# Attention layer of a decoder trunk: value units among the query units, halves swapped by the scalar engine, 16 partitions per sample, and idle matmuls over two waits

## The chip, the cores and the metric

The kernel runs on one core of one Trainium2 chip. A core has TensorE (PE: matmuls and transposes, results in PSUM), VectorE (DVE), ScalarE (ACT), GpSimd (POOL) and SyncE (SP, here only a queue that issues DMAs). Each runs its own instructions in order; they meet at semaphores. The metric is the device time in microseconds (us) of one launch; lower is better.

## The reference

One inference step of a two-layer decoder trunk, for a prompt of 256 tokens and 8 samples with one new token each. The kernel holds both as one set of 264 columns (T = 256 + 8). Layer 0 mixes tokens by sparse attention, layer 1 by a recurrent block; after each comes a gated MLP with a short convolution. Cut to the attention that the change touches:

```python
q, k, v, qi, ki, wi = split(a @ w_in)         # 8 heads of 128; indexer: 4 heads of 64, one key of 64
q, k, qi, ki = rope(q), rope(k), rope(qi), rope(ki)
# rope: x1, x2 = halves of a head; [x1*cos - x2*sin, x2*cos + x1*sin]
score = sum_h relu(qi_h . ki) * wi_h          # causal for the prompt; 257 keys for a sample
idx = top_k(score, 64)
o = softmax(q . k[idx] / sqrt(128)) @ v[idx]  # a sample takes its keys from a paged cache in DRAM
h = h + o @ w_out
```

For the prompt the kernel computes all logits and masks those that are not selected. For a sample it gathers 64 rows of the key cache and 64 of the value cache, and treats the new token's own key apart.

## The kernel before

Weights are float32 in DRAM. A unit is one 1024x128 block of a weight matrix (512 KB): SP loads it into one of four stages, ACT makes its float16 high part (`hi`, w_hi, L498), DVE the rest (`lo`, w_lo, L796), and PE multiplies 8 chunks of 128 rows by the 264 columns, three matmuls a chunk (L1263 to L1265; L1352 to L1354 where two or three units go chunk by chunk together), into PSUM bank u % 4. Stage, parts and bank are freed four units later, so load u waits for w_lo of u - 4, w_hi of u for unit u - 4, and unit u for the reader of bank u - 4.

The attention layer has 27 units in the order of `ORDER`: two of index queries (i0, i1), one of the index key and weights (w0), 8 of queries (q), 8 of keys (k), 8 of values (v). All but the value units are roped. DVE reads the bank three times (L882: times cos into its place; L884 and L886: each half times sin into the other half of `rot`; index units have four such halves), and POOL adds the two (L1658, semaphore roped). A value unit is copied by ACT (L589, L590).

All engines run a loop over u, and the work beside the units is hung into it by hand, by unit number. In this order:

- POOL issues 16 gathers of cached index keys (`kx`, L1593), sets constants, and only then begins the additions. After unit 4 PE waits for three roped units and computes the index scores (L1376 to L1391); after unit 6 it transposes the index keys.
- DVE sums the weighted scores (L1004, L1010) and takes the 64 largest in eight rounds of eight: `take_second` for tokens 128 to 255 (L896, L897), `take_merged` for the others and the samples, with indices (L902 to L904). At u = 12 it turns the samples' indices into cache row numbers (to L1037, semaphore phys_done). PE transposes them (L1425), DVE casts them (gix), and POOL gathers cached keys and values (L1651).
- SP writes the samples' queries to DRAM (L422) and reads them back broadcast over partitions (L380), 64 partitions a sample, two samples in a tile, in a buffer for two tiles; tiles 2 and 3 wait until DVE has read tiles 0 and 1. `sample_dots` (L929, L931, L933) multiplies them by the gathered keys and sums, at u = 16 to 19. PE transposes the dots after unit 19 (L1446).
- The prompt's heads start at LG = 17, one head a unit: logits on PE (L1322, L1323), masked row maximum on DVE (L914), exponentials on ACT (L560), normalising on POOL (L1671), transposes (L1329 to L1331) and output (L1339, L1340) on PE, output split on ACT and DVE (L571, L923). `TURNS` says after which unit a roped key or a value head is transposed for the store (L1313, L1314; kept by ACT, L580).
- The samples' value sums are PE's L1461, 8 matmuls a unit after units 22 to 25, with `pb`, the weights, two columns a tile; L1464 sums the weights. Then come the 8 units of w_out from 193.35 us.

Much later, after the 16 units of w_rec_in, the recurrent block's end makes z in 8 chunks (zH on ACT, zL on DVE, L1193), and the first two w_rec_out units take them chunk by chunk (L1352).

## Time and profile before

| what | value |
|---|---|
| time, median of 3 runs (lowest to highest) | 680.48 us (679.82 to 681.27) |
| the profiled execution: its time, its span | 684.84 us, 683.0 us |
| mean granted clock of TensorE | 0.933 |
| busy: PE, DVE, ACT, POOL | 598.2, 480.5, 350.5, 275.8 us |
| DMA | 115.42 MB, mean 169 GB/s |
| share of the chain that ended last: PE, DVE, issue, POOL, DMA | 56%, 17%, 14%, 5%, 4% |

The span runs from the first to the last instruction of the profiled execution. Busy time of PE is not PE at its peak, since matmuls are pipelined; the time between the starts of two matmuls says more than the length of one. The granted clock is 1.00 at full speed and 0.50 at half.

### The profile page before, as it was taken

The page shows a single profiled execution, that of the slowest core. Times are in us where ns is not written, and L with a number is a line of the kernel's source. Part 1 is how long each engine was busy: PE and PEld are TensorE (multiplying, and loading weights), DVE is VectorE, ACT ScalarE, POOL GpSimd, SP SyncE. Part 2 cuts the span into 40 slices and gives each one's busy share as a digit, 9 for nine tenths or more (in the row PEclk, how much of TensorE's full clock was granted, in tenths as well). Part 3 has the DMA queues.
Part 4 walks back from the last instruction along what each step waited for, and adds up shares of the span by engine and source line. Part 5 has one row for each costly group of instructions (what it writes and reads, how often), then busy time and mean ns, then how long its engine had stood idle before and what let it go on. Part 6 is the DMA issues. An engine that isn't in the chain of part 4 may idle for free.

```text
span 683.0 us, 12723 instructions
## 1 busy us (share of the span) xinstructions
PE 598.2 (88%) x5020; PEld 510.8 (75%) x5020; DVE 480.5 (70%) x876; ACT 350.5 (51%) x568; POOL 275.8 (40%) x275
## 2 busy tenths in 40 slices
PE   6869357369979999999999998948999999999995
PEld 5647246249867888888888887746888888888885
DVE  4569974576439888887865568797988778885442
ACT  6414204136427766665654458954776656663322
POOL 5843316127313354455400139983245545440001
PEclk9869759769999999999999999986999999999999
DMA  8833329913327876666876555542667666679601
GB/s 246 233 94 98 92 63 283 272 31 95 92 67 269 252 208 195 192 200 194 256 213 202 141 154 155 147 131 66 194 202 202 200 191 198 202 225 254 173 10 64
DMA packets 206076, 115.42 MB, mean 169 GB/s; under 512 B 5769, under 2 KB 202489, under 8 KB 205993
## 3 DMA queue, kind: packets, MB, share of 16 engines
q1 hardware_dynamic: 203601, 108.46, 56.1%
q0 software_dynamic: 2048, 5.79, 2.6%
q8 instruction: 40, 0.66, 0.4%
q10 hardware_dynamic: 368, 0.35, 0.2%
q14 instruction: 19, 0.16, 0.1%
HBM read 110.94 MB, written 3.90 MB: 168 GB/s over the span
## 4 chain that ended last, share of the span: by engine, by line
PE 56%; DVE 17%; issue 14%; POOL 5%; DMA 4%; ACT 4%; POOLq 1%; SPq 0%; ACTq 0%; DVEq 0%
PE acc L1263 16%; PE acc L1264 16%; PE acc L1265 16%; DVE w_lo L796 4%; DMA scratch<-q_rows 3%; POOL area L1593 3%; ACT w_hi L498 1%; DVE area L1179 1%; DMA pt<-in_page_table 1%; PE acc L1352 1%; DVE area L929 1%; DVE aL L803 1%; PE acc L1353 1%; PE acc L1354 1%; PE misc L1461 1%
## 5 line engine op out<-in xcount | busy, mean ns | idle before, releaser
L1263 PE MATMUL acc<-aH,w_hi 128*128 128x264 f16 (+1 forms) x1032 | 288.4, 279 | 1.1 <-DVE aL L803 0.8
L1264 PE MATMUL acc<-aL,w_hi 128*128 128x264 f16 (+1 forms) x1032 | 288.4, 279 | 0.0
L1265 PE MATMUL acc<-aH,w_lo 128*128 128x264 f16 (+1 forms) x1032 | 288.2, 279 | 0.0
L796 DVE SCALAR_TENSOR_TENSOR w_lo<-stage,w_hi 128x1024 f16<-128x1024 f32 (+1 forms) x179 | 235.0, 1316 | 52.8 <-ACT w_hi L498 52.2
L498 ACT ACTIVATE w_hi<-stage 128x1024 f16<-128x1024 f32 (+1 forms) x179 | 196.9, 1101 | 85.1 <-PE acc L1265 78.4
L1263 PE MATMUL acc<-zH,w_hi 128*128 128x264 f16 x440 | 121.5, 276 | 0.0
L1264 PE MATMUL acc<-zL,w_hi 128*128 128x264 f16 x440 | 121.4, 276 | 0.0
L1265 PE MATMUL acc<-zH,w_lo 128*128 128x264 f16 x440 | 121.4, 276 | 0.0
L1263 PEld LDWEIGHTS acc<-aH,w_hi 128*128 128x128 f16 (+1 forms) x1032 | 102.7, 99 | 19.2 <-issue 1.6
L1264 PEld LDWEIGHTS acc<-aL,w_hi 128*128 128x128 f16 (+1 forms) x1032 | 102.3, 99 | 17.6 <-issue 0.3
L1265 PEld LDWEIGHTS acc<-aH,w_lo 128*128 128x128 f16 (+1 forms) x1032 | 102.3, 99 | 16.3
L1647 POOL TENSOR_TENSOR scratch<-work,r0z 128x264 f32<-128x264 f32 x44 | 65.5, 1489 | 80.2 <-ACT work L700 80.2
L1645 POOL COPY ftail<-scratch 128x10 f32<-128x10 f32 x44 | 47.0, 1068 | 35.5 <-DVE scratch L1105 35.3
L1658 POOL TENSOR_TENSOR area<-area,scratch 128x264 f32<-128x264 f32 x16 | 26.4, 1649 | 73.2 <-DVE scratch L886 73.2
L695 ACT ACTIVATE work<-scratch,fprm 128x264 f32<-128x264 f32 x44 | 26.7, 607 | 52.0 <-DVE scratch L1105 51.8
L1263 PEld LDWEIGHTS acc<-zH,w_hi 128*128 128x128 f16 x440 | 43.0, 98 | 6.7 <-DVE w_lo L796 0.3
L1265 PEld LDWEIGHTS acc<-zH,w_lo 128*128 128x128 f16 x440 | 43.1, 98 | 6.4
L1264 PEld LDWEIGHTS acc<-zL,w_hi 128*128 128x128 f16 x440 | 43.1, 98 | 6.3
L1105 DVE TENSOR_TENSOR scratch<-acc,rinv 128x264 f32<-128x264 f32 x44 | 19.0, 432 | 39.5 <-PE acc L1265 39.4
L1577 POOL TENSOR_TENSOR sqsum<-sqsum,sq 128x264 f32<-128x264 f32 x21 | 16.8, 800 | 68.0 <-ACT sq L510 68.0
L700 ACT ACTIVATE work<-work 128x264 f32<-128x264 f32 x44 | 18.6, 423 | 34.9 <-DVE work L1116 34.9
L506 ACT ACTIVATE aH<-hT,gcol 128x264 f16<-128x264 f32 x24 | 12.3, 513 | 37.7 <-DVE hT L1135 23.2
(340 smaller groups left out, 742.4 us busy)
## 6 DMA issues: line engine op xcount, KB each, us to landing
stage<-in_w_ffn_up SPq DMA_DIRECT2D x88, 512.0 KB, 4.6
stage<-in_w_ffn_down SPq DMA_DIRECT2D x32, 704.0 KB, 5.0
stage<-in_w_attn_in SPq DMA_DIRECT2D x26, 512.0 KB, 4.3
stage<-in_w_rec_in SPq DMA_DIRECT2D x16, 512.0 KB, 4.0
stage<-in_w_attn_out SPq DMA_DIRECT2D x8, 512.0 KB, 3.7
stage<-in_w_rec_out SPq DMA_DIRECT2D x8, 512.0 KB, 3.7
scratch<-q_rows SPq DMA_DIRECT2D x8, 256.0 KB, 8.1
area<-in_x_prompt SPq DMA_DIRECT2D x2, 512.0 KB, 4.7
```

The costliest lines, as they stand in the source:

```text
L498: nc.scalar.activation(w_hi[:, s, 0:n, 0:cols], stage[:, s, 0:n, 0:cols], ACT.Copy, scale=WSCALE).then_inc(hi_done, 1)
L695: nc.scalar.activation(c32[:, p, :], gs[:, p, :], ACT.Identity, scale=fprm[layer][:, FROW_W + 2, j:j + 1], bias=fprm[layer][:, FROW_B, j:j ...
L700: nc.scalar.activation(c32[:, p, :], c32[:, p, :], ACT.Gelu_apprx_tanh).then_inc(gelu_done, 1)
L796: v.scalar_tensor_tensor(w_lo[:, s, 0:n, 0:cols], stage[:, s, 0:n, 0:cols], WSCALE, w_hi[:, s, 0:n, 0:cols], ALU.mult, ALU.subtract).then_ ...
L1105: v.tensor_tensor(gs[:, p, :], acc[:, u % 4, 0:T], rinv[:], ALU.mult).then_inc(acc_read, 1)
L1263: t_.matmul(out, w_hi[:, s, c, 0:cols], xH[:, x0 + c, :], start=first and c == 0, stop=False)
L1264: t_.matmul(out, w_hi[:, s, c, 0:cols], xL[:, x0 + c, :], start=False, stop=False)
L1265: ins = t_.matmul(out, w_lo[:, s, c, 0:cols], xH[:, x0 + c, :], start=False, stop=last and c == n - 1)
L1593: g.indirect_dma_start(out=kx[:, page, s * ID:(s + 1) * ID], out_offset=None, in_=kidx_rows, in_offset=bass.IndirectOffsetOnAxis(ap=gidx[: ...
L1645: g.tensor_copy(ftail[:, :, j], gs[:, p, TP - 2:T]).then_inc(tail_copied, 1)
L1647: g.tensor_tensor(gr[:, p, :], c32[:, p, :], r0z[:], ALU.mult).then_inc(gr_done, 1)
L1658: g.tensor_tensor(dst, dst, rot[0:part, (before(u) + 1) % 2, :], ALU.add).then_inc(roped, 1)
```

## The change

The core of the diff, by engine; the renumbering of steps that only move with the unit order is left out.

Order and buffers:

```diff
-ORDER = ("i0 i1 w0 q0 q1 q2 q3 q4 q5 q6 q7 "
-         "k0 v0 k1 k2 v1 k3 k4 v2 k5 k6 k7 v3 v4 v5 v6 v7").split()
+ORDER = ("i0 i1 w0 q0 q1 v0 q2 q3 v1 q4 q5 v2 q6 q7 v3 "
+         "k0 k1 k2 k3 k4 k5 k6 k7 v4 v5 v6 v7").split()
-TURN_K = (14, 15, 17, 18, 20, 21, 22, 28)
-TURNS = sorted([(U_V[h] + 1, "v", h) for h in range(H)] + [(TURN_K[h], "k", h) for h in range(H)])
+TURN_K = (17, 18, 19, 20, 21, 22, 23, 28)
+TURN_V = (8, 12, 13, 15, 24, 25, 26, 27)
+TURNS = sorted([(TURN_V[h], "v", h) for h in range(H)] + [(TURN_K[h], "k", h) for h in range(H)])
-        qb = scratch[:, 0:2048].rearrange("p (j d) -> p j d", j=2)
+        qb = scratch[:, 0:1024]
-        pb = sb("pb", [P, 4, H, 2])
+        pb = sb("pb", [P, 4, H, NS])
```

A sample now has 16 partitions, and its 64 keys lie in 4 tiles of 16; so one broadcast of all 8 queries serves all tiles. SP issues weight loads 4 to 6 ahead of the 21 parameter rows:

```diff
+            for u in range(4, 7):
+                load_in(u)
...
-            for u in range(4, U_OUT):
+            for u in range(7, U_OUT):
...
-                if u == 21:
+                if u == 23:
                     sp.wait_ge(smp_kept, 1)
                     sp.dma_start(q_rows, smp[:, 0, :]).then_inc(q_out, 16)
                     sp.wait_ge(q_out, 16)
-                    for j in range(2):
-                        broadcast_q(j)
-                if u in (24, 25):
-                    sp.wait_ge(qb_read, u - 23)
-                    broadcast_q(u - 22)
+                    sp.dma_start(qb, q_rows.rearrange("(s h) d -> s (h d)", h=H).unsqueeze(1).to_broadcast([NS, 16, D])).then_inc(qb_in, 16)
```

ACT swaps the halves, after the head's steps of that u and ahead of `hi(u + 4)`; DVE multiplies in place:

```diff
+            def swap_halves(u):
...
+                act.wait_ge(unit_done, u + 1)
+                if r > 2:
+                    act.wait_ge(roped, r - 2)
+                for b in range(0, rows_n, 2 * half):
+                    nc.scalar.copy(rot[b:b + half, r % 2, :], acc[b + half:b + 2 * half, s, 0:T])
+                    ins = nc.scalar.copy(rot[b + half:b + 2 * half, r % 2, :], acc[b:b + half, s, 0:T])
+                ins.then_inc(swapped, 1)
...
-                v.tensor_tensor(dst, acc[0:rows_n, s, 0:T], cos[0:rows_n, :], ALU.mult)
-                for b in range(0, rows_n, 2 * half):
-                    v.tensor_tensor(rot[b:b + half, r % 2, :], acc[b + half:b + 2 * half, s, 0:T],
-                                    sin[b + half:b + 2 * half, :], ALU.mult)
-                    ins = v.tensor_tensor(rot[b + half:b + 2 * half, r % 2, :], acc[b:b + half, s, 0:T],
-                                          sin[b:b + half, :], ALU.mult)
-                ins.then_inc(acc_read, 1)
+                dve.wait_ge(swapped, r)
+                v.tensor_tensor(rot[0:rows_n, r % 2, :], rot[0:rows_n, r % 2, :], sin[0:rows_n, :], ALU.mult)
+                v.tensor_tensor(dst, acc[0:rows_n, s, 0:T], cos[0:rows_n, :], ALU.mult).then_inc(acc_read, 1)
```

DVE's steps: the wait for three roped units and the placing of the index queries (`qz`, 4 copies instead of 8) come ahead of rope 3 instead of behind w_lo 7. Score sums go to u = 7, `take_second` to u = 8 (3 rounds), 9 and 10 (2 each) and 15 (1), `take_merged` to u = 11 to 14 (2 rounds each), the row numbers to u = 14, `sample_dots` from 16 to 19 to 18 to 21. `lane` and `own` are two new reduces of the identity at u = 5. Addresses and weights:

```diff
+                    small(v.tensor_tensor(picked.rearrange("p (n r) -> p n r", r=16), C[:, 0:P].rearrange("p (n r) -> p n r", r=16),
+                                          lane[:].unsqueeze(1).to_broadcast([P, 8, 16]), ALU.mult))
+                    small(v.tensor_reduce(gbias[:], picked.rearrange("p (n r) -> p n r", r=16), AX.X, ALU.add))
+                    v.tensor_copy(gix[:], gbias[:, 0:4]).then_inc(gix_done, 1)
...
+                    v.tensor_tensor(pb[:].rearrange("p j h s -> p (j h) s"), E[:, 0:32].unsqueeze(2).to_broadcast([P, 32, NS]),
+                                    own[:].unsqueeze(1).to_broadcast([P, 32, NS]), ALU.mult)
```

PE: idle matmuls (`keep_warm`, whose result nobody reads), the first two units staggered, and the value sums:

```diff
+            keep_warm(acc[:, 2, 0:P], 14)
+            for c in range(DC):
+                a_ready(0)(c)
+                chunk(0, c, aH, aL)
+                if c in (0, 1):
+                    keep_warm(acc[:, 2, 0:P], 4)
+                else:
+                    chunk(1, c - 2, aH, aL)
...
-                if u == 12:
+                if u == 15:
...
+                    t_.matmul(C[:, 0:P], of_sample[:], pf, start=True, stop=True).then_inc(phys_turned, 1)
...
-                if 22 <= u < 26:
-                    j = u - 22
+                if u in (24, 25):
                     pe.wait_ge(pb_done, 1)
...
+            pe.wait_ge(gate_tanh, 2 * DC)
+            keep_warm(A[:, 0:P], 80)
             units_together(U_ROUT, 2, zH, zL, lambda c: pe.wait_ge(y_lo, c + 1))
```

The other steps on PE move with them: index scores from after unit 4 to after 5, key transposes from 6 to 7, sample scores from 7 and 8 to 9 and 10, parameter transposes from 9 to 11, the dots' transposes from 19 to 21.

POOL sets its constants first, gathers 8 of the 16 index key pages, and issues the other 8 in pairs after additions 1 to 4; the key and value gathers move from u = 13 to 16 to u = 16 to 19:

```diff
+            gather_index_keys(0, 8)
...
+                if 1 <= u < 5:
+                    gather_index_keys(6 + 2 * u, 2)
-                if 13 <= u < 17:
-                    pool.wait_ge(gix_done, 2)
+                if 16 <= u < 20:
+                    pool.wait_ge(gix_done, 1)
```

## Rows read from the trace of the kernel before

**Rows 1.** Busy time by stretch: PE, PEld, DVE, ACT, POOL; clock, DMA, GB/s.

```profile
0.00:44.50 44.50, 29.36 (x197) 24.41 (x198) 25.80 (x53) 19.96 (x36) 28.21 (x39) 0.81 0.75 208
44.50:93.30 48.80, 29.21 (x227) 22.80 (x226) 42.65 (x112) 13.23 (x21) 14.23 (x8) 0.78 0.36 94
93.30:145.30 52.00, 30.09 (x205) 24.19 (x205) 31.24 (x61) 13.78 (x29) 19.51 (x17) 0.76 0.73 197
145.30:193.35 48.05, 43.29 (x334) 37.76 (x334) 26.59 (x90) 23.10 (x67) 19.14 (x29) 0.93 0.27 79
```

**Rows 2.** Instructions in order of time on PE: start us, length us, line, tiles.

```profile
160.61 0.39 PE L1322 MATMUL misc<-area 128*128 128x128 f32 x2
160.83 0.60 PE L1323 MATMUL misc<-area 128*128 128x256 f32 x2
...
473.27 0.28 PE L1263 MATMUL acc<-zH,w_hi 128*128 128x264 f16 x1
473.38 0.28 PE L1264 MATMUL acc<-zL,w_hi 128*128 128x264 f16 x1
```

**Rows 3.** PE's waits from 0 to 200 us: total us, times, longest.

```profile
PE misc L1322 <- DVE nmx L914: 18.5, 2, 11.1
PE misc L1425 <- DVE zL L1037: 12.8, 1, 12.8
PE misc L1376 <- issue: 7.7, 1, 7.7
```

**Rows 4.** Groups of POOL, 0 to 200 us: busy us, mean ns, idle before.

```profile
L1658 POOL TENSOR_TENSOR area<-area,scratch 128x264 f32<-128x264 f32 x16 | 26.4, 1649 | 73.2 <-DVE scratch L886 73.2
L1593 POOL DMA_INDIRECT area<-in_cache_kidx,gidx x16 | 19.1, 1196 | 4.9 <-issue 4.6 <-POOL gidx L1588 0.3
```

**Rows 5.** Instructions in order of time, all engines, near 35 us.

```profile
34.91 1.44 POOL L1658 TENSOR_TENSOR zH<-zH,scratch 128x264 f32<-128x264 f32 x2
35.76 0.42 DVE L882 TENSOR_TENSOR zH<-acc,ca 64x264 f32<-64x264 f32 x1 [5.81 <-POOL zH L1658]
```

**Rows 6.** Groups of ACT, 0 to 200 us.

```profile
L498 ACT ACTIVATE w_hi<-stage 128x1024 f16<-128x1024 f32 (+1 forms) x31 | 32.4, 1044 | 48.2 <-PE acc L1265 41.5 <-DMA stage<-in_w_attn_in 6.7
L560 ACT ACTIVATE work<-work,nmx 128x128 f32<-128x128 f32 (+1 forms) x16 | 7.1, 449 | 32.5 <-DVE nmx L914 32.5
L590 ACT ACTIVATE scratch<-acc 128x264 f32<-128x264 f32 x8 | 3.1, 382 | 0.0
```

**Rows 7.** The tile q_rows: its DMA issues, and time to landing.

```profile
L380 SPq DMA_DIRECT2D scratch<-q_rows x8: 445/596/3477, 105.7 to 126.7; - x8
...
DMA to landing us min/median/max: 3.6/7.8/10.2
```

**Rows 8.** Groups of DVE from 52.6 to 93.3 us.

```profile
L796 DVE SCALAR_TENSOR_TENSOR w_lo<-stage,w_hi 128x1024 f16<-128x1024 f32 x7 | 8.6, 1226 | 0.2
...
L884 DVE TENSOR_TENSOR scratch<-acc,ca 64x264 f32<-64x264 f32 x6 | 2.6, 434 | 0.1
...
L896 DVE MAX8 top<-zH 128x8 f32<-128x256 f32 x6 | 2.6, 427 | 0.2
```

**Rows 9.** Groups of all engines from 97 to 145 us.

```profile
L929 DVE TENSOR_TENSOR area<-scratch,area 128x1024 f32<-128x1024 f32 x4 | 5.4, 1356 | 12.4 <-DMA scratch<-q_rows 12.4
...
L931 DVE TENSOR_REDUCE qk<-area 128x8 f32<-128x1024 f32 x4 | 4.9, 1220 | 0.1
```

**Rows 10.** Instructions in order of time on PE, value sums and last wait.

```profile
162.25 1.84 PE L1461 MATMUL misc<-pb,area 128*128 128x2 f32 x16
...
191.59 0.48 PE L1313 MATMUL misc<-ca,scratch 128*128 128x128 f32 x1 [4.16 <-DVE zL L923]
```

**Rows 11.** Instructions in order of time on PE, first output unit of the recurrent block.

```profile
463.23 0.40 PE L1352 MATMUL acc<-zH,w_hi 128*128 128x264 f16 x1 [10.83 <-DVE zL L1193]
463.43 0.43 PE L1353 MATMUL acc<-zL,w_hi 128*128 128x264 f16 x1
463.65 0.43 PE L1354 MATMUL acc<-zH,w_lo 128*128 128x264 f16 x1
```

**Rows 12.** Instructions in order of time on DVE, the last two parts zL.

```profile
468.69 1.00 DVE L1193 TENSOR_TENSOR zL<-work,zH 128x264 f16<-128x264 f32 x2
```

More of the change, by code:

```diff
@@ L1276, in _ @@
             pe.wait_ge(ones_set, 1)
-            for _ in range(WARM):
-                t_.matmul(acc[:, 0, 0:P], ones[:], ones[:], start=True, stop=True)
+            keep_warm(acc[:, 0, 0:P], WARM)
             pe.wait_ge(const_in, 16)
```

260 lines of the change are left out of this document (131 added, 129 removed).

## The prediction

> **What bounds the kernel now.** I read the busy time by stage first [rows 1]. From 193 us on (both FFN layers and the recurrent block) TensorE, PE from here, is busy nearly without a break at full clock, but for one hole near 460 us. The attention layer, the first 193.35 us, is different: PE is busy 29 us of each of its first three stretches of 44 to 52 us, and its mean clock there is 0.76 to 0.81. Its 27 projection units need 24 matmuls each at 0.11 us [rows 2], 2.7 us a unit, 73 us in all; the rest of the stage is waiting. PE's waits name what for [rows 3]: 7.7 us before the transposes of L1376 (the third rope), 12.8 us for the gather addresses that VectorE (DVE) works out (L1037), 18.5 us for the row maxima of the logits (L914), which stand behind the query-key products on DVE's queue. So three chains in a row set the stage: GpSimd (POOL) at the start, DVE from 45 to 93 us, then a DMA and DVE up to the transposes of the dots at 145.3 us. The change shortens each; I follow them as clock readings and compare with those of before.
>
> **Start, to the index matmuls.** POOL issues 16 gathers of index keys at 1.2 us, plus 0.3 us between two, before it does anything else [rows 4]; they hold it from 9.6 to 33.3 us, the rope additions queue behind them, and DVE's third rope starts at 35.76 [rows 5]. With 8 gathers it is free near 21.8. The idle matmuls hold PE's first unit to a steady start at full clock, where they now run partly at half clock; a float matmul of 128 columns takes 0.22 us warm (two instructions between 160.61 and 160.83) [rows 2], so 14 of them end at 14.9, 4 and 4 more at 16.1 and 17.3, and the first two units end at 21.0 and 22.0, not 23.1: 1 us earlier.
> A rope before is three DVE instructions of 0.43 us beside one POOL addition; after, ScalarE (ACT) copies the two halves crosswise out of PSUM and DVE does two. The nearest row for a copy is the value units' one of 128x264, 0.38 us, the next instruction following 0.27 us later [rows 6]. I take 0.27 a copy: 0.55 us for a query or key unit, 1.1 us for an index unit, done before the weight split w_hi, 1.04 us in the mean and 0.95 to the next instruction, on the same queue. So unit end to rope end goes from 1.34 to 0.6 + 0.9 = 1.5 us, but DVE's own share falls from 1.34 to 0.89. Bounds for a copy: 0.27 and 0.38 us if each waits for the last; I keep both for the range, plus more in a rival.
> Then: first rope done on DVE 23.7, second 25.8, third 27.9; POOL adds them at 24.4, 27.5 and, after two gathers (2.5 us, the time of two late ones), 30.75. Before, the third was added at 38.9. DVE now waits at this point ahead of rope 3 and its w_lo; they end at 34.7, and unit 7, which needs that w_lo, starts at 37.8, so nothing is late. Index matmuls: from 32.8 (unit 5 is done by then) to 34.9 at full clock, against 44.46 with one unit less done. Parameter rows now go out behind three weight loads: load 7 leaves at 25.3 instead of well before; its w_hi is wanted at 31, and it lands near 30.
> The new wait is for the index keys themselves: the last two gathers go out behind rope additions 3 and 4 and their issue ends at 40.8, landing near 43 (my estimate is 2 us; the nearest row, the query rows' way to DRAM and back, gives 3.6 as the shortest [rows 7], so 44.5 is the upper bound); PE is there at 40.5. So 2.5 us idle; unit 8 ends at 47.2.
>
> **Selection, to the gather addresses.** This is DVE alone: busy 42.65 of 48.8 us before [rows 1]. From its rope at 52.65 to the addresses at 93.0 it works 40.4 us. After: five ropes of 0.89 instead of six of 1.34 (-3.6), one w_lo of 1.15 more, one selection round more (two DVE instructions, 0.99), one flag and one doubled address less (-0.35): 38.6 us [rows 8]. It starts at 41.2 and waits once, 1 us, for unit 8's w_hi; the addresses stand at 81.0, against 93.3. PE idles from 70.8 to 81.0 and restarts at half clock, as it does before in the stretch after 93.3 (mean clock 0.76 [rows 1]); I charge unit 16 with 5.4 us. The two reduces for lane and own fall into a gap of DVE at 38 us; each is under one 256-wide selection instruction (0.43 us), so without that gap they cost 0.3 to 0.9 us.
>
> **Query broadcast and dots.** The new form needs one product, one reduce and one cast of at most 128 columns (0.8 us, between two and three times 0.43) for the addresses and one broadcast for all samples. Load 23 waits for w_lo 19, done 82.4; the query rows leave at 83.0, land 3.6 us later, and the single 512 KB broadcast goes out at 86.8. Before, eight of 256 KB took 7.8 us in the median and up to 10.2 to land [rows 7], and the second half waited for a free buffer. I take 7.8 us, the median: 94.6. Bounds: 5 and 10.2 us; DVE comes to it only at 97.6, after logits 0 and rope 18, so only the upper one can touch it. Key rows are issued at 90.2 and land near 98.5. From there DVE goes round one loop per unit: logits 0.55, ACT's exponentials 0.9 and swap 0.55, rope 0.9, w_lo 1.15 to the next instruction (1.23 by itself), dots 1.23 + 1.22 + 0.2 [rows 6, 8, 9], 6.9 us with gaps. Here the swap is a cost: it stands behind the exponentials on ACT, and DVE's rope behind it. Four rounds: the last dot at 122.0. PE waits 3 to 5 us in each round, hidden behind DVE. So the transposes move from 145.3 to 122.1; this piece is 41.1 us instead of 52.0.
> The Trainium skill speaks against the one broadcast: its page DMA: Bandwidth & Descriptors, section Rules for kernel authors, says that an outermost dimension under 16 confines a DMA to that many engines, and this source has 8 outermost. By it the transfer runs on half the engines; no row of before has such a shape (those broadcasts have 64 outermost), so this is a rival below.
>
> **Tail.** Two units fewer are left (5, not 7): -5.4 us. Unit 22 is now a key unit, so PE waits 2 us at the token-major transpose for the output split behind rope 22. The value sums: 32 matmuls of two instructions over two units instead of four, 64 instructions either way (16 take 1.84 us with the last one's latency [rows 10]), and six more instructions for the weight sum, 0.7 us; the wider N is free. From unit 26 to the last head nothing is touched: the wait of 4.16 us before 191.59 stays [rows 10]. Readings: units 22, 23, 24, 25, 26 end at 128.4, 134.9, 140.2, 148.3, 156.9; output projection at 164.0, not 193.35. That piece is 41.9 instead of 48.05.
>
> **Recurrent output.** PE waits there 10.83 us and resumes at 463.23, at half clock (0.2 us a matmul) [rows 11]. The change puts 80 float matmuls there, 80 x 0.22 = 17.8 us warm, from 452.2 to 470.0. The last zL is done at 469.7 [rows 12], so all eight chunks are then ready: 48 x 0.112 = 5.4 us, the pair ends at 475.4 instead of 473.27. PE has no gap behind it for 200 us, so +2.1 us stay. Bounds: +1.6 if a pass takes 0.107 us, and -2.9 if the idle matmuls ended before the first zL: the chunks would then keep pace with the zL, and the pair end 0.7 us after the last of them, at 470.4.
> The Trainium skill's page TensorE: Matmul & The Clock Gate, section Why this matters for your kernels, says to leave no idle gap between bursts, which taken alone gives a gain here. The row bears out the half clock after the gap, but not that filling it past its end is free: that rule gives -2.9, my sum +2.1.
>
> **Sum.** Addresses -12.3, broadcast and dots -10.9, tail -6.1, idle matmuls +2.1: -27.2 us. The profiled execution spans 683.0 us and took 684.8, 4.4 above the median of 680.5; so the -27.2 us are applied to the median: 653.3 us.
>
> **Rivals.** (1) Less comes through, 662 us: the POOL-DVE pair slows both (a POOL addition takes 1.65 us in the mean and 0.72 alone [rows 4, 5]), rope's first product now has both operands in SBUF, and each of the four rounds and some of the first units lose 1 to 1.5 us, some waits push PE to half clock at unit 8. For: such additions overlap w_lo often. Against: DVE's own rows hardly stretch. (2) The broadcast on half the engines (the first page named above would have it): twice the longest landing, 20.4 us, gives 107 instead of 98.5, 662 us. Against: it goes out while the DMA queues are light, and twice the median is 102, +4. (3) More comes through, 647 us: the idle matmuls pay (-2.9) or the rounds run nearer 6 us since exponentials overlap. (4) Slower than before, 690 us: ACT's queue becomes the ring. A swap waits for the rope two before, and w_hi stands behind it; if copies between partition halves cost over 1.0 us each, then 19 units lose 1.4 us each and the gain is gone. That is the point; at 1.3 us it is 690. Against: 0.38 us in the only such row, though between the same partitions. (5) The edits hide behind each other and nothing moves, 680: would need the selection chain to start no earlier, against the 7.7 us wait.
>
> **How the numbers follow.** Forecast 0.58; (1) 0.13; (2) 0.08; (3) 0.16; (4) 0.04; (5) 0.01. The predicted time is the forecast's, 653.3 us. The range takes in (1), (2) and most of (3) and the bounds of copies and landing: 643 to 665. Faster by over 0.2% (about what a measurement of this kernel can tell from no change) 0.95, same 0.01, slower 0.04.
>
> **What would show it.** In the changed profile: POOL's third rope addition near 31; the address matmul near 81 with PE idle 10 us before it; a wait of 2 to 3 us for index keys near 41; four rounds of 6.9 us ending near 122; the first output unit at 164; the 160 idle instructions in one block that ends 5.4 us ahead of the pair's last matmul. Wrong if a swap copy costs over 0.4 us, if rounds exceed 8 us, or if the broadcast lands after 98 us.

## The result, and the profile after the change

The changed kernel takes 663.03 us in the median of 6 runs (660.95 to 670.87), against 681.67 us for the kernel before beside it (679.82 to 684.74). The ratio is 0.9732, with a 95% interval from 0.9702 to 0.9763: 18.3 us faster, two thirds of the 27.2 forecast. (The ratio leaves out the changed kernel's slowest run, 670.87 us, which is also its profiled one.) The prediction, 653.3 us, is too low by 9.7; the time lies in its range.

The profiled execution has a span of 669.1 us and a mean granted clock of 0.957, where the runs near the median had 0.972 to 0.975. The reading below is made against its own span, 13.9 us under the 683.0 of before. It is 7.8 us above the median, so part of what the pieces below miss belongs to this one execution; the changed kernel has no other trace, and how much it is can only be told from kernels that share its code in a stretch (see the table of the experiments and the part on the tail).

Busy time by stretch in the changed kernel, cut at the same events as [rows 1]; the last line is the stretch from the last unit of the recurrent block to the end of the pair of output units. Columns: stretch, its length, busy time of PE, PEld, DVE, ACT, POOL, then clock, DMA share, GB/s.

```profile
0.00:35.70 35.70, 32.30 (x265) 29.53 (x266) 20.67 (x39) 24.89 (x48) 22.59 (x35) 1.00 0.89 241
35.70:86.00 50.30, 36.26 (x280) 28.79 (x280) 42.04 (x109) 23.39 (x48) 14.97 (x12) 0.87 0.50 131
86.00:128.50 42.50, 30.03 (x199) 24.35 (x200) 32.44 (x66) 19.78 (x47) 24.99 (x23) 0.82 0.62 197
128.50:177.10 48.60, 42.45 (x269) 35.81 (x270) 20.75 (x73) 17.93 (x52) 13.41 (x24) 0.78 0.19 57
436.20:459.50 23.30, 23.30 (x211) 22.57 (x210) 16.37 (x29) 5.40 (x11) 10.53 (x11) 1.00 0.30 91
```

The first line ends where the index products end. The start keeps the full clock now (0.81 in [rows 1]) and is 8.8 us shorter. The second stretch is no shorter than before: 50.3 against 48.8 us, with one more unit in it; DVE is busy 42 us of it in both. The third gains 9.5 us. The fourth has two units fewer and yet is 0.5 us longer; its clock is 0.78 against 0.93. As readings:

| event, us | before | forecast | changed kernel |
|---|---|---|---|
| index products done | 44.5 | 34.9 | 35.7 |
| address product | 93.3 | 81.0 | 86.0 |
| transposes of the sample dots | 145.3 | 122.1 | 128.5 |
| output projection starts | 193.35 | 164.0 | 177.1 |
| last recurrent unit to the end of the pair (length) | 21.0 | 23.2 | 23.3 |

The forecast missed 0.8 us in the first piece, 4.2 in the second, 1.4 in the third, 6.7 in the fourth and 0.1 at the pair: 13.2 us, which is the difference between -27.2 and -13.9 but for 0.1.

PE's waits from 0 to 200 us in the changed kernel (us in total, times, longest), which answer to [rows 3]:

```profile
PE misc L1441 <- DVE zL L1037: 9.3, 1, 9.3
PE misc L1325 <- DVE nmx L918: 9.3, 4, 3.6
PE misc L1316 <- DVE zL L927: 6.1, 2, 4.2
PE misc L1414 <- DMA area<-in_cache_kidx,gidx: 4.5, 1, 4.5
```

The 7.7 us before the third rope's transposes are gone, the wait for the addresses fell from 12.8 to 9.3, that for the row maxima from 18.5 to 9.3, and a wait for the index keys is new. It is the first of three places where the missing time lies. In order of time on POOL and PE:

```profile
41.08 1.40 POOL L1626 DMA_INDIRECT area<-in_cache_kidx,gidx  x1 [0.30 <-issue]
...
46.43 1.94 PE L1414 MATMUL misc<-ca,area 128*128 128x128 f32 x8 [4.46 <-DMA area<-in_cache_kidx,gidx]
48.16 0.43 PE L1262 MATMUL acc<-aH,w_hi 128*128 128x264 f16 x1
```

The last gather's issue ends at 42.48, the keys are there at 46.4, 3.9 us later. Units ran with 0.28 us a matmul before the wait; here they show 0.43, one starting every 0.22 us: the clock has fallen to its lower level, 1.2 GHz. Unit 8 lasts from 48.16 to 53.04, 4.9 us instead of 2.9. DVE's chain of selection stands behind the high part that ACT makes once unit 8 is done:

```profile
54.59 1.23 DVE L807 SCALAR_TENSOR_TENSOR w_lo<-stage,w_hi 128x1024 f16<-128x1024 f32 x1 [5.37 <-ACT w_hi L494]
```

The forecast had 1 us for this wait; it is 5.4.

The second place is the round of the sample dots. One round on DVE, and then the same part of it on ACT:

```profile
106.21 0.28 DVE L918 CUSTOM_DVE_ANT_0 work<-misc,zH 128x128 f32<-128x128 f32 x1
...
106.42 0.42 DVE L918 CUSTOM_DVE_ANT_0 work<-misc,zH 128x256 f32<-128x256 f32 x1
...
108.33 0.43 DVE L891 TENSOR_TENSOR scratch<-scratch,ca 128x264 f32<-128x264 f32 x1 [1.49 <-ACT scratch L589]
108.68 0.42 DVE L892 TENSOR_TENSOR area<-acc,ca 128x264 f32<-128x264 f32 x1
109.03 0.15 DVE L923 RECIPROCAL prcp<-psum_e 128x2 f32<-128x2 f32 x1
109.41 1.60 DVE L807 SCALAR_TENSOR_TENSOR w_lo<-stage,w_hi 128x1024 f16<-128x1024 f32 x1 [0.23 <-ACT w_hi L494]
110.94 1.21 DVE L933 TENSOR_TENSOR area<-scratch,area 128x1024 f32<-128x1024 f32 x1
112.18 1.22 DVE L935 TENSOR_REDUCE qk<-area 128x8 f32<-128x1024 f32 x1
```

```profile
106.53 0.40 ACT L556 ACTIVATE work<-work,nmx 128x128 f32<-128x128 f32 x1 [4.26 <-DVE nmx L918]
...
106.93 0.49 ACT L556 ACTIVATE work<-work,nmx 128x256 f32<-128x256 f32 x1
107.33 0.19 ACT L556 ACTIVATION_READ_ACCUMULATOR work<-work,nmx 128x1 f32 x1
107.54 0.38 ACT L588 COPY scratch<-acc 64x264 f32<-64x264 f32 x1
107.93 0.37 ACT L589 COPY scratch<-acc 64x264 f32<-64x264 f32 x1
```

The products of the dots start at 103.57, 110.94, 118.33 and 125.70: rounds of 7.37 us. In each, ACT stands 4 us, gets the maxima, does 1.0 us of exponentials and only then 0.8 us of copies, although the unit that they copy has long been done; DVE stands 1.49 us for both. Also, w_lo takes 1.60 us in each round, not 1.23: it starts 0.2 us into POOL's addition of the same rope:

```profile
109.19 0.74 POOL L1684 TENSOR_TENSOR area<-area,scratch 128x264 f32<-128x264 f32 x1 [2.43 <-DVE area L892]
```

The two copies start 0.39 us apart and the next instruction begins 0.4 us behind the second: copies do not overlap.

The third place is the tail. The fourth stretch again, cut at its units (22 to 26, then the last wait):

```profile
128.50:134.60 6.10, 6.06 (x28) 3.96 (x28) 2.04 (x7) 0.99 (x5) 0.00 (x0) 0.53 0.05 14
134.60:143.00 8.40, 6.45 (x39) 5.30 (x40) 4.24 (x15) 4.42 (x12) 5.75 (x10) 0.80 0.22 62
143.00:148.50 5.50, 5.50 (x47) 4.87 (x46) 2.83 (x9) 3.44 (x11) 2.15 (x5) 1.00 0.30 89
148.50:158.10 9.60, 9.60 (x70) 8.29 (x69) 5.47 (x25) 3.41 (x10) 4.48 (x8) 0.82 0.20 60
158.10:170.00 11.90, 11.90 (x78) 10.93 (x77) 2.37 (x6) 2.66 (x7) 1.04 (x4) 0.71 0.16 45
170.00:177.10 7.10, 2.94 (x15) 2.45 (x14) 3.80 (x11) 2.99 (x9) 0.00 (x0) 0.86 0.26 75
```

PE is busy throughout the fourth and fifth lines, and its clock is 0.82 and 0.71 there: it works, but part of the time at half clock.

### The profile page after: what moved, and what is told of

It reads as the page before. It is cut to its first block, busy times and chain, and to the rows that moved or that the text cites. A ratio compares the mean times of both kernels' runs of the same rounds, so it can differ in the third digit from the quotient of the medians.

```text
span 669.1 us, 13155 instructions
## 1 busy us (share of the span) xinstructions
PE 621.2 (93%) x5230; PEld 536.4 (80%) x5230; DVE 470.1 (70%) x847; ACT 366.4 (55%) x610; POOL 270.6 (40%) x275
## 4 chain that ended last, share of the span: by engine, by line
PE 62%; issue 13%; DVE 11%; ACT 6%; POOL 3%; DMA 3%; SPq 1%; POOLq 1%; ACTq 0%; DVEq 0%
PE acc L1262 17%; PE acc L1263 17%; PE acc L1264 17%; DVE w_lo L807 3%; PE misc L1270 3%; ACT w_hi L494 2%; POOL area L1626 1%; PE misc L1480 1%; DMA stage<-in_w_ffn_up 1%; SPq L377 1%; DMA area<-in_x_prompt 1%; DMA area<-in_cache_kidx,gidx 1%; DVE qk L935 1%; DVE area L933 1%; PE acc L1352 1%
## 5 line engine op out<-in xcount | busy, mean ns | idle before, releaser
L807 DVE SCALAR_TENSOR_TENSOR w_lo<-stage,w_hi 128x1024 f16<-128x1024 f32 (+1 forms) x179 | 238.2, 1334 | 58.2 <-ACT w_hi L494 57.9
L494 ACT ACTIVATE w_hi<-stage 128x1024 f16<-128x1024 f32 (+1 forms) x179 | 196.8, 1101 | 39.9 <-PE acc L1264 37.0
L1262 PEld LDWEIGHTS acc<-aH,w_hi 128*128 128x128 f16 (+1 forms) x1032 | 103.0, 100 | 19.6 <-DVE aL L814 1.1
L706 ACT ACTIVATE work<-scratch,fprm 128x264 f32<-128x264 f32 x44 | 26.7, 607 | 52.2 <-DVE scratch L1104 51.9
L1684 POOL TENSOR_TENSOR area<-area,scratch 128x264 f32<-128x264 f32 x16 | 18.5, 1157 | 57.8 <-DVE area L892 57.7
L502 ACT ACTIVATE aH<-hT,gcol 128x264 f16<-128x264 f32 x24 | 12.3, 513 | 39.9 <-DVE hT L1134 23.2
```

Of the source, the lines that this page charges most:

```text
L494: nc.scalar.activation(w_hi[:, s, 0:n, 0:cols], stage[:, s, 0:n, 0:cols], ACT.Copy, scale=WSCALE).then_inc(hi_done, 1)
L706: nc.scalar.activation(c32[:, p, :], gs[:, p, :], ACT.Identity, scale=fprm[layer][:, FROW_W + 2, j:j + 1], bias=fprm[layer][:, FROW_B, j:j ...
L807: v.scalar_tensor_tensor(w_lo[:, s, 0:n, 0:cols], stage[:, s, 0:n, 0:cols], WSCALE, w_hi[:, s, 0:n, 0:cols], ALU.mult, ALU.subtract).then_ ...
L1262: t_.matmul(out, w_hi[:, s, c, 0:cols], xH[:, x0 + c, :], start=first and c == 0, stop=False)
L1684: g.tensor_tensor(dst, dst, rot[0:part, (before(u) + 1) % 2, :], ALU.subtract).then_inc(roped, 1)
```

## The experiments

Each kernel is the changed one but for its edit. Medians come from 4 to 6 runs and ratios are to the kernel before on the same chip. The single edits of 3 to 5 us are hardly to be told apart in them, since each ratio has an interval 0.6 to 1.5% wide; so the lengths of stretches in each profiled execution stand beside them. Start: when the index products begin. Selection: from there to the address product. Dots: to the transposes of the sample dots. Tail: to the end of the wait of 4.16 us at the last head. Pair: from the last recurrent unit to the end of the pair. All in us.

| kernel | median | ratio (95%) | start | selection | dots | tail | pair |
|---|---|---|---|---|---|---|---|
| before | 681.7 | | 41.6 | 51.8 | 51.9 | 46.3 | 21.0 |
| changed | 663.03 | 0.9732 (0.9702 to 0.9763) | 34.2 | 51.9 | 42.5 | 46.9 | 23.3 |
| warm56 | 663.26 | 0.9736 (0.9694 to 0.9779) | 39.1 | 50.0 | 43.5 | 40.7 | 18.3 |
| warm0 | 665.82 | 0.9753 (0.9696 to 0.9811) | 37.8 | 50.3 | 43.9 | 44.1 | 19.6 |
| swap_first | 664.71 | 0.9764 (0.9721 to 0.9808) | 34.4 | 52.3 | 39.4 | 43.3 | 23.3 |
| dve_rope | 668.33 | 0.9815 (0.9759 to 0.9871) | 34.0 | 54.8 | 39.9 | 44.0 | 23.3 |
| later_keys | 664.41 | 0.9735 (0.9663 to 0.9807) | 33.9 | 48.3 | 43.8 | 44.1 | 23.3 |
| no_start_warm | 665.77 | 0.9745 (0.9670 to 0.9821) | 34.3 | 50.4 | 43.8 | 44.1 | 23.3 |
| loads_back | 669.19 | 0.9797 (0.9724 to 0.9871) | 36.0 | 50.3 | 43.8 | 44.1 | 23.3 |
| all_three | 658.43 | 0.9646 (0.9589 to 0.9704) | 40.7 | 46.6 | 40.7 | 44.1 | 18.3 |
| three | 655.67 | 0.9642 (0.9597 to 0.9687) | 37.4 | 46.6 | 39.7 | 43.3 | 18.3 |
| three_cold | 651.13 | 0.9584 (0.9538 to 0.9629) | 34.7 | 46.6 | 39.8 | 43.4 | 18.4 |
| three_sums | 658.84 | 0.9701 (0.9660 to 0.9741) | 35.0 | 46.6 | 41.0 | 44.1 | 18.3 |
| three_waits | 653.56 | 0.9609 (0.9574 to 0.9644) | 34.1 | 46.3 | 40.1 | 40.8 | 18.3 |

From the end of the tail to the pair all of them take about 261 us, and from the pair to the last matmul 202.5 us. The pair column moves only with the idle matmuls ahead of it. The start, by contrast, varies by up to 6.8 us between kernels whose code up to that point is the same. From the address product on, the changed kernel, warm56, warm0, later_keys, no_start_warm and loads_back are the same code up to the pair: dots take 43.5 to 43.9 us in the other five against its own 42.5, the tail 44.1 in four and 40.7 in one against its own 46.9.

**Fewer idle matmuls at the recurrent pair: warm56.**

```
-            keep_warm(A[:, 0:P], 80)
+            keep_warm(A[:, 0:P], 56)
```

> 56 idle matmuls instead of 80 ahead of the recurrent output pair; nothing else differs from the changed kernel. In the changed kernel's trace the 80 took 17.85 us (436.05 to 453.90) and the last of the eight zL pieces that the pair waits for was there at 453.5, so 56 of them end 12.5 us after the last unit and the pair goes with the pieces (0.69 us apart, as its six matmuls at full clock take 0.68), ending at 454.2 instead of 459.4. Theory (80 are too many, by the part behind the first piece): 5.1 us faster than the changed kernel, some 658 us, 0.965 of the kernel before. Rival (the clock falls anyway in the gap between two pieces, or the pair pays something else): 1 us or less, 662 us.

The stretch, here and in the kernel below:

```profile
434.60:452.90 18.30, 18.11 (x162) 16.64 (x162) 16.33 (x29) 5.41 (x11) 10.40 (x11) 1.00 0.30 89
```

18.3 us against 23.3: the 5.0 us are there in this stretch, at full clock throughout. The median did not follow, as this execution began its index products 5 us later; the time of the kernel as a whole leaves this open, the stretch does not.

**None: warm0.**

```
-            keep_warm(A[:, 0:P], 80)
```

> No idle matmuls ahead of the recurrent output pair, as in the kernel before. Theory by my sum (80 cost 2.1 us more than they give): 2.1 us faster than the changed kernel, 661 us, 0.970. Rival by the rule that no idle gap should be left (they pay 2.9 us): 2.9 us slower than the changed kernel, 666 us. The pair should end 21.0 us behind the last unit, at half clock for most of it, against 23.2 in the changed kernel.

```profile
437.20:456.70 19.50, 7.81 (x51) 5.72 (x52) 16.23 (x29) 5.42 (x11) 10.31 (x11) 0.65 0.33 100
```

19.6 us, at a clock of 0.65: the idle matmuls cost 3.7 us against this run and 2.3 against the kernel before; the clock came back somewhat sooner here. By the stretch the theory holds and the rival falls; the medians (665.8 and 663.0, intervals overlapping) can't tell. With warm56 the order is plain: idle matmuls pay 1.3 to 2.7 us where they end with the wait, and cost 2.3 to 3.7 where they run on behind it.

**The copies of the halves ahead of the exponentials: swap_first.** From unit 18 on, `swap_halves(u)` stands before `exp_scores`:

```
+                if LG + 1 <= u < U_OUT and u not in U_V:
+                    swap_halves(u)
                 if LG + 1 <= u < LG + 1 + H:
                     exp_scores(u - LG - 1)
...
-                elif u < U_OUT:
+                elif u <= LG:
                     swap_halves(u)
```

> From unit 18 on ScalarE copies the swapped halves ahead of the two exponentials of the head, not behind them. In the changed kernel's trace VectorE stands 1.49 us in each of the four rounds of the sample dots, between the logits and the rope, while ScalarE does 1.0 to 1.1 us of exponentials and then 0.76 us of copies; the rounds are 7.37 us apart. Theory (the place of the copies in ScalarE's order makes the rounds long): the wait of 1.49 goes, the weight split waits some 0.7 us longer for its high half, rounds of 6.5 us, 3.2 to 4 us faster than the changed kernel, 659 to 660 us, 0.968. Rival (TensorE sets the rounds, by the logits that wait for the maxima and the values behind them): same as the changed kernel within 1 us, 663 us, with the same 7.4 us between rounds.

DVE in one round:

```profile
107.59 0.43 DVE L893 TENSOR_TENSOR scratch<-scratch,ca 128x264 f32<-128x264 f32 x1
107.94 0.43 DVE L894 TENSOR_TENSOR area<-acc,ca 128x264 f32<-128x264 f32 x1
108.39 0.17 DVE L925 RECIPROCAL prcp<-psum_e 128x2 f32<-128x2 f32 x1
109.33 1.27 DVE L809 SCALAR_TENSOR_TENSOR w_lo<-stage,w_hi 128x1024 f16<-128x1024 f32 x1 [0.78 <-ACT w_hi L494]
110.52 1.21 DVE L935 TENSOR_TENSOR area<-scratch,area 128x1024 f32<-128x1024 f32 x1
```

The 1.49 us are gone, 0.78 us for the high half came, as expected; the rounds are 6.1, 6.6 and 6.2 us, the dots stretch 39.4 us instead of 42.5 to 43.9. POOL's addition now ends before w_lo begins, and w_lo is back at 1.2 to 1.4 us. The place of the copies in ACT's order set the rounds; PE did not. In the median of the single edit (664.7 us) it doesn't show.

**The rope on DVE alone: dve_rope.** Its rotation has the sign opposite to the reference's, as POOL still subtracts; the instructions are those of the kernel before.

```
-                dve.wait_ge(swapped, r)
-                v.tensor_tensor(rot[0:rows_n, r % 2, :], rot[0:rows_n, r % 2, :], sin[0:rows_n, :], ALU.mult)
-                v.tensor_tensor(dst, acc[0:rows_n, s, 0:T], cos[0:rows_n, :], ALU.mult).then_inc(acc_read, 1)
+                v.tensor_tensor(dst, acc[0:rows_n, s, 0:T], cos[0:rows_n, :], ALU.mult)
...
```

> The rope goes back to VectorE alone: three products that read the accumulator, two of them across the partition halves, and no copies by ScalarE; all else as in the changed kernel. Theory (the swap gives little, since its two copies take 0.38 us each one after the other, 0.76 a unit and 1.5 for an index unit, where the forecast had 0.27 each): VectorE's work grows by 0.4 us or so per query and key unit, but its wait of 1.49 us in the rounds goes; within 1.5 us of the changed kernel, 662 to 665 us. Rival by the forecast (the swap takes VectorE's work off the path in the address and dot stages): 6 to 9 us slower than the changed kernel, 669 to 672 us, 0.984.

Neither number: 5.3 us slower in the median, between the two. The stretches say why. Selection is 54.8 us, 2.9 us longer than in the changed kernel and 2.5 to 4.8 longer than in the other runs with the key transposes in the same place: there the swap pays. Dots is 39.9 us, 2.6 to 4 us shorter: there, behind the exponentials, it costs what it saved. With the copies ahead of the exponentials (39.4) it costs nothing.

**Index-key transposes behind unit 8: later_keys.** `if u == 7` becomes `if u == 8` on PE and `u == 8` becomes `u == 9` on ACT, and the first entry of `TURN_V` 9.

> The transposes of the gathered index keys stand behind unit 8 instead of unit 7 (their copy by ScalarE and the first value turn one unit later too). In the changed kernel's trace TensorE waits 4.5 us for the keys at 41.97, its clock has fallen by 45.4, the transposes take 1.9 us and unit 8 4.9 us instead of 2.9, and the split of unit 12's weights, with the selection behind it on VectorE, starts at 54.6. Theory (the late keys delay the selection): unit 8 runs in the wait, no wait of over 1.5 us there, the stretch from the index products to the address product is 51.8 us in the changed kernel and becomes 47 to 48; 4 us faster than the changed kernel, 0.967. Rival (VectorE's own work fills the stretch, as it waits elsewhere for the same keys): stretch of 51 to 52 us, same time.

```profile
PE misc L1414 <- DMA area<-in_cache_kidx,gidx: 2.2, 1, 2.2
```

Selection is 48.3 us against 51.9 (50.0 to 52.3 in the five other runs with the old place and the copies on ACT), the remaining wait 2.2 us. So the late keys and the slow unit behind them did delay the chain on DVE, by 1.7 to 4 us of the miss of 4.2 in this piece. The median, 664.4 us, shows nothing of the edit.

**No idle matmuls around the first pair: no_start_warm.**

```
-            keep_warm(acc[:, 2, 0:P], 14)
...
-                if c in (0, 1):
-                    keep_warm(acc[:, 2, 0:P], 4)
-                else:
+                if c >= 2:
```

> The changed kernel without its idle matmuls around the first pair of units (14 ahead, 4 behind each of the first two pieces). Theory (they hold the clock through the stage's start, at some cost in the pair): without them the clock falls in the waits for the first pieces and the first units run at half clock as in the kernel before; the index products start 2.5 to 4 us later than the 34.0 of the changed kernel's profiled run, 665.5 us, 0.977. Rival (they are many instructions ahead of the stage: in two profiled runs of variants TensorE stood 1.7 and 2.1 us with nothing to wait for between them, and the index products began at 37.8 and 39.1): without them the start is at 34 to 35 in every run, and the kernel is 0 to 3 us faster than the changed one, 661 us.

The index products begin at 34.3 us. The clock does fall (mean 0.91 up to 36.2 us in the kernel three_cold below, which has the same start), but little is lost by it, as the first pieces wait for DVE anyway. The rival's start came true, its gain in the median did not.

**Loads of units 4 to 6 back behind the parameters: loads_back.**

```
-            for u in range(4, 7):
-                load_in(u)
...
-            for u in range(7, U_OUT):
+            for u in range(4, U_OUT):
```

> The weight loads of units 4 to 6 go back behind the parameter loads in SyncE's order, as in the kernel before; the rest is the changed kernel's. Theory (loads ahead of the parameters keep the first units fed and are worth 0 to 1 us, by the forecast): units 4 to 7 wait for their weights, index products 1 us later, 0 to 1 us slower than the changed kernel. Rival (three more loads of 512 KB crowd the queues when the index keys are gathered, 4 us from issue to landing instead of 2, and when instructions are fetched): keys land 2 us earlier, TensorE's wait of 4.5 us for them becomes 2.5, 2 us faster, 661 us.

The keys land hardly sooner: 3.5 us behind the end of the last issue instead of 3.9, and PE waits 4.0 us for them. The rival's 2 us are out. The start is 2.1 us later than the earliest, more than the theory's 1 us, but this execution also has some of the gaps told of below; the median is 6 us higher, more than either said.

**All three edits: all_three.** As warm56 and later_keys, and the copies together with the next `hi(u + 4)` ahead of the exponentials.

> Three edits on the changed kernel together: 56 idle matmuls instead of 80 ahead of the recurrent pair; index-key transposes behind unit 8; and from unit 18 on the copies of the halves and the high half of the next weights ahead of the exponentials on ScalarE. Measured so far in traces: the first shortened its stretch by 5.0 us (18.3 against 23.3), the copies alone ahead of the exponentials shortened address product to sample transposes from 42.5 (43.5 and 43.9 in two variants) to 39.4 with a wait of 0.78 us a round left for the high half. Theory (each acts on its own stretch, and they add): rounds of 5.6 us, that stretch 36.5 to 37.5, together 5.0 + 6 + 4 = 15 us faster than the changed kernel, 648 us, 0.951. Rival (what one gains the next stage gives back, since the timed runs of the single edits were no faster than the changed kernel): 658 to 661 us, 0.968.

Two of the three add up as told (46.6 and 18.3 us). The dots stretch is 40.7, not 37. Its rounds are 5.2, 9.2 and 5.2 us: two as short as told, and one in which DVE waits 2.2 us for the copies of a unit that took PE 4.9 us at half clock, and 1.2 us for exponentials. In the first round the exponentials stand behind the high half (1.06 us) and a table load (1.28 us), and DVE's reciprocal 2.6 us behind them; I took that for a wait for weights in the next expectation, which the trace of ACT doesn't bear out. And this execution shows best what moves the start; PE in order of time:

```profile
17.65 0.27 PE L1356 MATMUL acc<-aH,w_hi 128*128 128x264 f16 x1 [0.48 <-issue]
19.07 0.38 PE L1357 MATMUL acc<-aL,w_hi 128*128 128x264 f16 x1 [1.15 <-issue]
20.53 0.38 PE L1358 MATMUL acc<-aH,w_lo 128*128 128x264 f16 x1 [1.08 <-issue]
```

Three consecutive matmuls, whose operands are there, start over 1 us apart, with no releaser in the profile; then PE runs at half clock to 25.9 us. In the changed kernel's own trace the same three follow each other every 0.11 us. Such gaps (1.2 to 2.7 us in sum) stand between 17 and 22 us in five of the eleven executions with the idle matmuls at the start (warm56, warm0, loads_back, all_three, three), and in neither of the two without. What PE waits for the profile doesn't name. Late instructions are my guess; it was not tested.

**The three edits with the high half left in its place: three.**

> Three edits on the changed kernel: 56 idle matmuls instead of 80 ahead of the recurrent pair, index-key transposes behind unit 8, and from unit 18 on the copies of the halves alone ahead of the exponentials (the next high half stays behind them; where it stood ahead, it waited 2.6 us for its weights with the exponentials behind it). Theory (the edits act on separate stretches and add): by the traces of the single edits, key transposes to address product 34 to 34.5 us (37.6 in the changed kernel), then 39.4 to the sample transposes (42.5 to 43.9), then 18.3 for the recurrent pair (23.3): 12 us faster than the changed kernel in the stretches, about 651 to 653 us in the median, 0.957. Rival (the clock and the start take part of it back, as they seem to have done in the single runs): 658 us, 0.966.

655.67 us, ratio 0.9642: between theory and rival. The stretches are as the theory has them (46.6, 39.7, 18.3); the start of the profiled execution is 3.2 us later than the changed kernel's.

**The same without the idle matmuls at the start: three_cold.**

> As the one with three edits, and without the idle matmuls around the first pair of units. Theory (they buy next to nothing, as without them the index products began at 34.3 against 34.0, though TensorE had stood 2.4 us for its instructions): the same time within 1 us as the one with three edits in good starts and 3 to 4 us faster in starts in which instructions come late, the median 1 to 2 us lower. Rival (they keep the clock up, as meant): 2 to 3 us slower than the one with three edits.

651.13 us, 4.5 below the kernel beside it, the lowest time of this study: 0.9584 of before. Its profiled start is 34.7 us. The 2.4 us that the expectation speaks of, in no_start_warm, were waits for the pieces of aL: this trace names them so (2.2 us in two waits), and in both traces PE resumes 0.1 us behind the same two pieces. The intervals of the two ratios overlap (0.9538 to 0.9629 and 0.9597 to 0.9687), so that the idle matmuls of the start cost 4.5 us isn't shown; that they don't pay 2 us, as the rival has it, is.

**One idle matmul behind each head's value sums: three_sums.**

```
                             t_.matmul(E[:, 64 + 8 * h:72 + 8 * h], vgat[:, j, h * P:(h + 1) * P], pb[:, j, h, :],
                                       start=j == 0, stop=j == 3)
+                        keep_warm(E[:, 328:456], 1)
```

> As the one with three edits, and behind the four value-sum matmuls of each head, which have 8 columns, one idle float matmul of 128 columns: 8 in all, 1.8 us. In the traces so far the clock is at half for 3.4 us in the unit behind each block of 32 value sums (units 25 and 26, 4.5 us instead of 2.9), and in the kernel before, where the sums stood in four blocks of 16 by 2 columns, it was not. Theory (a block of narrow matmuls brings the clock down): no low clock behind the sums, units 25 and 26 of 2.9 us, minus 3.2 plus 1.8: 1 to 1.5 us faster than the one with three edits, and the spells gone in its trace. Rival (the spells have another cause): still there, 1.8 us slower.

Unit 25 behind the sums, in three_sums and then in the kernel with three edits alone:

```profile
145.70:150.30 4.60, 4.60 (x28) 3.44 (x28) 1.30 (x9) 0.99 (x4) 2.40 (x7) 0.63 0.00 1
```

```profile
148.50:153.10 4.60, 4.60 (x28) 3.45 (x28) 2.28 (x14) 0.98 (x4) 1.49 (x4) 0.63 0.21 62
```

The same clock of 0.63, the same 4.6 us. My theory falls in this form: one wide matmul in five doesn't keep the clock, and the kernel is 3.2 us slower (the intervals overlap by a little). Nor do the sums alone bring it down: unit 25 ran at full clock in three_waits and in warm56, and unit 26, behind the second block, did so in swap_first, three and three_cold. In no execution of the changed kernel or its variants were both at full clock; in the kernel before none of the units behind its four blocks was slow. What decides it is open.

**Idle matmuls in two waits of PE: three_waits.**

```
+                    keep_warm(A[:, 0:P], 38)
                     pe.wait_ge(phys_done, 1)
...
+                    keep_warm(E[:, 0:P], 12)
                     pe.wait_ge(qb_read, 4)
```

> As the one with three edits, and idle float matmuls in two waits of TensorE: 38 ahead of the address product (8.4 us of a wait of 9.4) and 12 ahead of the sample transposes (2.6 us of a wait of 2.5 to 3.3). Theory (the clock is at half behind these waits because TensorE stands in them): unit 16 in 2.9 us instead of 4.0, unit 22 in 2.9 to 3.5 instead of 4.5 to 5.3, with the turns behind it 1 us shorter; of the first nothing reaches the end, since VectorE and the gathers set that stretch, the second does: 2 to 4 us faster than the one with three edits. Rival (the levels follow something else): units 16 and 22 as before, the same time.

The wait for the last dots and unit 22, with them and (second fence) in the kernel without:

```profile
116.60:120.50 3.90, 2.87 (x26) 2.68 (x25) 3.79 (x4) 1.04 (x3) 2.69 (x2) 1.00 0.41 123
120.50:123.80 3.30, 3.29 (x28) 2.62 (x28) 2.04 (x7) 0.00 (x0) 0.00 (x0) 1.00 0.06 19
```

```profile
120.50:123.60 3.10, 0.54 (x3) 0.24 (x1) 3.00 (x4) 1.04 (x3) 1.90 (x1) 0.50 0.45 134
123.60:129.50 5.90, 5.83 (x28) 3.85 (x28) 2.04 (x7) 0.00 (x1) 0.00 (x0) 0.56 0.06 18
```

Unit 22 with its transposes takes 3.3 us instead of 5.9, unit 16 2.9 instead of 4.1. The tail is 40.8 us instead of 43.3, the median 2.1 us lower, both as the theory has it, though the intervals of the two ratios overlap. Idle matmuls pay where PE waits anyway and what follows it is PE's own work. These two waits filled and the start left cold were not run together.

## Why the prediction was right or wrong

**The start: right.** The third rope addition is at 31.3 us (forecast 30.75), the index products end at 35.7 (34.9), at full clock. This is where the gain up to the addresses comes from: the index products begin 7.5 us earlier than before, and from them to the address product it takes 51.9 us against 51.8. That it is the split of the 16 gathers that does it, and the one broadcast that shortens the dots, is read from the traces (the third addition at 31.3 us and not 38.9, no wait of DVE for the broadcast); neither was taken back in a run of its own.

**The copies: the lower bound was taken, the upper one was true.** 0.27 us a copy was read as the time to the next instruction of a value copy [rows 6]. The new ones hold ACT for 0.38 us each, one after the other:

```profile
L588 ACT COPY scratch<-acc 64x264 f32<-64x264 f32 (+1 forms) x21 | 7.8, 374 | 16.9 <-PE acc L1264 14.9 <-PE acc L1354 1.6 <-POOL zH L1684 0.2
L589 ACT COPY scratch<-acc 64x264 f32<-64x264 f32 (+1 forms) x21 | 7.8, 370 | 0.2
```

That is 0.2 us more a unit, and 0.4 for an index unit; it stays under the 0.4 us a copy that would have made the forecast wrong, and far from the 1.0 of the fourth rival.

**The index keys: the term that failed in the second piece.** The forecast had the last issue's end at 40.8 us, 2 us to landing, a wait of 2.5, and unit 8 ending at 47.2 at full clock. Measured: 42.5 (the additions between the gathers took up to 1.6 us and the gathers up to 1.8), 3.9 us to landing, a wait of 4.5 and unit 8 ending at 53.0 at half clock. The 3.6 us of [rows 7] were named as a bound and were the better value. So DVE stood 5.4 us for unit 8's high part, where the forecast had 1. Of the 5.8 us, 5.0 arrive at the address product; later_keys took 1.7 to 4 back by letting unit 8 run in the wait.

**Selection itself: right.** From w_lo at 54.6 us to the address product at 86.0 DVE has no wait worth naming, and PE stands 9.3 us before it (forecast 10).

**Broadcast and dots: right but for the rounds.** The broadcast is issued 5.6 us behind the address product (forecast 5.8), and DVE reaches the first dot without a wait for it, 11.9 us later. Four rounds were put at 6.9 us each and take 7.37; three of them, 1.4 us, are the whole miss of this piece. The exponentials and copies, on which DVE stands, were put at 1.45 us and cost 1.49: the copies took 0.2 us more, the rest less. The terms that were too small are w_lo, 1.15 us in the forecast and 1.53 to the next instruction here, beside POOL's addition, and the 0.38 us of a reciprocal and of waiting for the high part, which it left out; rope took 0.2 us less than its 0.9. swap_first shows what the order costs on top, and that 6.1 to 6.6 us are to be had.

The rival of the broadcast on half of the engines can't be read from the end of a wait, since there is none. While it has the queues nearly to itself, from 93.2 to 96.0 us, the engines' mean share is 0.52:

```profile
93.20:96.00 2.80, 2.80 (x25) 2.42 (x24) 1.78 (x2) 1.31 (x5) 2.42 (x2) 1.00 0.52 140
```

The Trainium skill has it that an outermost dimension of 8 confines a transfer to at most 8 of the 16 engines (page DMA: Bandwidth & Descriptors, section Rules for kernel authors). A share of 0.52 agrees with that. It proves little, and the price that I gave the rival, 4 to 8 us, was not paid: DVE comes to the first dot so late that the transfer had 12 us.

**Tail: the work right, the clock wrong.** The forecast was 41.9 us, measured 48.6. The waits are as forecast (1.99 us behind the rope of unit 22, 4.16 at the last head), and so is the first block of value sums (3.5 us; the second took 4.6, half of it at half clock). But the forecast took the tail at the clock of before, 0.93 [rows 1]; here it is 0.78. Three traces with the same code in this stretch, from the transposes of the dots to the end of the last wait (changed kernel, no_start_warm, warm56):

```profile
128.48:175.34 46.86, 40.71 (x264) 34.32 (x264) 20.59 (x73) 17.62 (x52) 13.41 (x24) 0.79 0.19 56
128.43:172.57 44.14, 37.99 (x264) 32.25 (x264) 20.94 (x73) 17.61 (x52) 14.26 (x24) 0.85 0.21 59
132.58:173.28 40.70, 34.55 (x263) 30.02 (x264) 20.61 (x73) 17.63 (x51) 15.36 (x24) 0.92 0.23 66
```

PE is idle for 6.15 us in each, and the length times the clock is 37.0 to 37.5 us in all three: only the clock differs. At the 0.93 of before these 37.3 us would take 40.1, and with the 1.8 us up to the output projection 41.9, the forecast. So the step was mis-sized by a clock that the changed kernel doesn't keep. Of the 6.7 us, 2.8 are of this execution alone, since four others took 44.1. Where PE stood before unit 22 the cause is shown (three_waits filled that wait and took 40.8 us); for the spells of half clock behind the value sums no cause is shown.

**Idle matmuls at the pair: right.** +2.1 us forecast, +2.3 measured. The rule of leaving no idle gap between bursts (the Trainium skill, TensorE: Matmul & The Clock Gate, section Why this matters for your kernels), taken by itself, would have a gain, which the prediction put at -2.9; warm56, in which they end with the wait, has -2.7 against before. Rule and sum are both true, each at its own count.

**The rivals.** The first, 662 us, names the time that came, but only half of its mechanism: the half clock at unit 8 was there and w_lo was slower beside POOL, but the rounds lost 0.5 us and not 1 to 1.5, and the loss in the tail was in no rival; that the time agrees is in part luck. The third did not come; rounds near 6 us and idle matmuls that pay 2.7 us can be had, but by edits of their own (651 us in three_cold). The fourth and the fifth are out.

## What to carry to other kernels

Read the queue order of the helper engine before giving it work: a copy that could have been done early, put behind an instruction that waits for the consumer's own result, costs the consumer the copy and the wait. Idle matmuls are worth their place only up to the end of the wait that they fill, and most where PE's own work follows; count them from the trace, not by feel. A forecast for a stretch that PE bounds needs its clock as a term of its own: the same instructions took 40.7 to 46.9 us here.

## What the runs showed of the hardware

- A matmul whose operands are there can start over 1 us late with nothing in the profile to name the cause: three in a row at 17 to 21 us in all_three, whose index products began 6.8 us later than the earliest with the same instructions. Gaps of this kind came in five of eleven executions.
- ACT's copies out of PSUM into other partitions, 64x264 float, take 0.37 to 0.38 us each, and the next one doesn't begin before the last has ended; each costs about as much as the straight copy of twice the partitions, 128x264 (0.38 us [rows 6]).
- The last gather of index keys, 128 rows, was there 2.9 to 4.0 us after the end of its issue in the thirteen traces (3.9 in the changed kernel), and an issue takes 0.9 to 2.0 us of POOL.
- The granted clock was at half in the unit behind the first block of value sums in eleven of thirteen executions, and behind the second in ten, with the same instructions from the sums on but for one; a matmul of 128 columns in every five did not change it.
- w_lo, 128x1024, takes 1.60 us in the rounds where it starts 0.2 us into an addition on POOL, and 1.2 to 1.4 in swap_first, where that addition has ended. In the kernel before it takes 1.23 with an addition beside it for 1.18 us, so overlap alone isn't the cause; no run isolates it.
